# Router products among the last out-projection's, expert 0's rows in two parts, expert 1's rows among expert 0's products

## The reference

```
[u,q,k,v] = rmsnorm(x) @ w_in
x  = x + concat(pool(u), diff_attention(q,k,v)) @ w_out
h2 = rmsnorm(x)
g  = argmax(h2 @ w_group + b_group)                # 1 of 4 groups
e  = top 2 of the 4 experts of group g, by h2 @ w_erouter + b_erouter
moe = sum over the 2 chosen experts: weight * (silu(h2 @ w_gate[e]) * (h2 @ w_up[e])) @ w_down[e]
y  = rmsnorm(x + moe)
```

## Time and profile before

| what | value |
|---|---|
| three runs | 442.7, 442.85, 444.68 us; median 442.85 |
| profiled execution: span from the first to the last instruction | 441.1 us |
| median less span (what lies around the span, and scatter) | 1.75 us |
| PE busy | 416.4 us, 94% of the span |
| DVE busy | 273.4 us, 62% |
| ACT busy | 197.9 us, 45% |
| POOL busy | 124.1 us, 28% |
| mean granted TensorE clock | 0.990 of full speed |
| DMA | 91.36 MB, mean 207 GB/s; 346 to 409 GB/s in nearly all slices from 254 to 386 us |

### The profile page before, as it was taken

How to read it: one execution, slowest core, us unless ns; L and a number is a source line. 1 busy time by engine, 2 the same in 40 slices (tenths; PEclk the granted TensorE clock), 3 DMA queues, 4 the chain that set the end, 5 groups by cost and what they waited for, 6 DMA issues and landing times.

```text
span 441.1 us, 7798 instructions
## 1 busy us (share of the span) xinstructions
PE 416.4 (94%) x2932; PEld 364.6 (83%) x2933; DVE 273.4 (62%) x655; ACT 197.9 (45%) x485; POOL 124.1 (28%) x207
## 2 busy tenths in 40 slices
PE   6899999999999999999999999999999999999970
PEld 2686999997876777788886899999989999998950
DVE  2856230806769898554357898555577777659870
ACT  5476320705665756332223534444555555547340
POOL 2010000200133416242001304333344555545231
PEclk9999999999999999999999999999999999999995
DMA  8851704406000059913225699999999999984120
GB/s 269 295 179 49 227 2 128 171 1 198 2 1 3 1 212 393 369 55 145 96 97 201 192 364 392 375 409 364 348 364 346 362 346 353 366 303 151 58 78 21
DMA packets 32073, 91.36 MB, mean 207 GB/s; under 512 B 11200, under 2 KB 11712, under 8 KB 27942
## 3 DMA queue, kind: packets, MB, share of 16 engines
q1 hardware_dynamic: 20790, 71.97, 44.0%
q0 software_dynamic: 11248, 18.93, 12.1%
HBM read 86.38 MB, written 26.01 MB: 255 GB/s over the span
## 4 chain that ended last, share of the span: by engine, by line
PE 73%; DMA 11%; DVE 7%; ACT 4%; issue 3%; POOLq 0%; POOL 0%; SPq 0%; DVEq 0%; ACTq 0%
PE ps L1191 20%; PE ps L823 10%; PE ps L825 9%; PE ps L824 9%; DMA region_w<-in_w_down 5%; DMA region_x<-h_rows,lists 5%; PE ps L1208 2%; PE ps L1209 2%; PE ps L1213 2%; PE ps L1184 2%; PE ps L979 2%; PE ps L1125 2%; PE ps L944 2%; DMA region_x<-in_x_prompt 1%; PE ps L962 1%
## 5 line engine op out<-in xcount | busy, mean ns | idle before, releaser
L1191 PEld LDWEIGHTS ps<-region_p,region_a 128*128 128x128 f32 x512 | 58.2, 192 | 1.1 <-DVE region_p L2028 0.4
L1191 PE MATMUL ps<-region_p,region_a 128*128 128x128 f32 x512 | 58.6, 275 | 0.0
L825 PE MATMUL ps<-region_a_r,region_w_r 128*128 128x288 f32 x192 | 56.5, 294 | 0.0
L823 PE MATMUL ps<-region_a_r,ring_r 128*128 128x288 f32 x128 | 40.5, 317 | 0.0
L824 PE MATMUL ps<-region_a_r,ring_r 128*128 128x288 f32 x128 | 37.7, 295 | 0.0
L825 PEld LDWEIGHTS ps<-region_a_r,region_w_r 128*128 128x128 f32 x192 | 36.0, 188 | 0.0
L1578 ACT ACTIVATE region_p<-ps,gffn_sb 128x128 f32<-128x128 f32 x116 | 31.6, 384 | 8.3 <-PE ps L1184 8.3
L1599 ACT ACTIVATE region_t<-ps 128x256 f32<-128x256 f32 x16 | 6.1, 384 | 56.6 <-PE ps L1191 56.6
L1191 PEld LDWEIGHTS ps<-region_p,region_w 128*128 128x128 f32 x256 | 29.1, 192 | 1.4 <-issue 1.2
L1191 PE MATMUL ps<-region_p,region_w 128*128 128x128 f32 x256 | 29.3, 275 | 0.8 <-DMA region_w<-in_w_down 0.8
L1191 PEld LDWEIGHTS ps<-region_p,ring 128*128 128x128 f32 x256 | 29.1, 192 | 0.8 <-DVE region_p L2050 0.5
(11 more groups left out here) (358 smaller groups left out, 1022.8 us busy)
## 6 DMA issues: line engine op xcount, KB each, us to landing
region_a<-in_w_gate SPq DMA_DIRECT2D x8, 1024.0 KB, 9.6
region_a<-in_w_up SPq DMA_DIRECT2D x8, 1024.0 KB, 17.4
region_a<-in_w_down SPq DMA_DIRECT2D x8, 1024.0 KB, 18.1
region_w<-in_w_in SPq DMA_DIRECT2D x2, 2048.0 KB, 10.2
region_w<-in_w_out SPq DMA_DIRECT2D x2, 2048.0 KB, 8.0
ring<-in_w_gate SPq DMA_DIRECT2D x4, 1024.0 KB, 8.6
ring<-in_w_up SPq DMA_DIRECT2D x4, 1024.0 KB, 17.1
ring<-in_w_down SPq DMA_DIRECT2D x4, 1024.0 KB, 12.5
```

What stands on the lines that cost most here:

```text
L823: pe.matmul(out, lhs_hi, rhs_hi, start=first, stop=False)
L825: return pe.matmul(out, lhs_lo, rhs_hi, start=False, stop=last)
L1191: ins = pe.matmul(ps[:, 2 + b, (first + c) * P:(first + c + 1) * P], w[:, k, c * P:(c + 1) * P], xT[:, b, k, :], start=(k == 0), stop=(k = ...
```

## The change

- PE runs the router's products and transposes of tiles 2 and 3 earlier among the out-projection's matmuls. Six of the eight features of the last half of tile 4 go ahead of the rank matmuls of the prompt, the last two behind them. DVE and ACT evacuate to match; `residual(4, 1)` goes behind the first one-hot rows.
- Expert 0's gathered rows are plain transposes, scaled by ACT (8 chunks). The sample rows get two PSUM banks of their own (`LATE_BANK`), and DVE adds them chunk by chunk; `gate_up(0)` waits for each chunk (`first_sum`).
- The third token list and expert 1's transposes go between expert 0's groups of products; `rows_out(1)` goes ahead of the table's last steps; the first two lists go between the third and the fourth group of expert 1 (`first_lists`).
- Three `keep_running` calls go. `wd_los(0)` goes behind `lists_out(1)`; ACT's `wd_his(0)` goes behind `silu(0)`.
- Two pairs of semaphores are merged (`gains_loaded`, `ov_passed`), with the same order of work.

```diff
@@ PE, after transpose_h2(0) @@
-            for t in range(2, NT):
-                project_out(t, 0, (*heads, *pools))
-                router_logits(t - 2)
-                if t < NT - 1:
-                    project_out(t, 1, (*heads, *pools))
-                transpose_h2(t - 1)
-            project_out(NT - 1, 1, heads)
-            router_logits(NT - 2)
-            project_out(NT - 1, 1, pools)
-            pe.wait_ge(h2T_dve, PT)
-            pe.wait_ge(h2T_act, PT)
-            keep_running(2, 4)
+            project_out(2, 0, (*heads, *pools))
+            router_logits(0)
+            project_out(2, 1, (*heads, *pools))
+            transpose_h2(1)
+            project_out(3, 0, (*heads, *pools))
+            router_logits(1)
+            transpose_h2(2)
+            project_out(3, 1, heads)
+            router_logits(2)
+            project_out(3, 1, pools)
+            project_out(NT - 1, 0, heads)
+            transpose_h2(3)
+            project_out(NT - 1, 0, pools)
+            router_logits(3)
+            project_out(NT - 1, 1, (*heads, *pools[0:2]))
             pe.wait_ge(mask_ready, 1)
...
             ins.then_inc(rank_full, 1)
-            keep_running(4, 4)
-            transpose_h2(NT - 1)
-            pe.wait_ge(early_onehot, 1)
+            project_out(NT - 1, 1, pools[2:4])
+            pe.wait_ge(onehot_late, 1)
             for t in range(PT):
                 ins = pe.matmul(ps[:, 6, 0:2], onehot_all[:, 0, t, :], tokv[:, t, :], start=(t == 0), stop=(t == PT - 1))
             ins.then_inc(idx_full, 1)
+            keep_running(4, 4)
+            transpose_h2(NT - 1)
             keep_running(2, 4)
             router_logits(NT - 1)
...
             ins.then_inc(rank_full, 1)
-            keep_running(3, 4)
@@ PE, gate_up: waits by chunk, and work between the groups @@
                         for k in range(KC):
+                            if by_chunk is not None and first + c == 0:
+                                pe.wait_ge(by_chunk, k + 1)
                             ins = pe.matmul(...)
+                        for at, work in between:
+                            if at == first + c:
+                                work()
@@ PE, first_rows @@
-                for b in range(2):
-                    pe.matmul(ps[:, b, :], ones[:, :], ..., start=True, stop=False)
...
                 pe.wait_ge(xg_loaded[0], 16)
...
-                        ins = pe.matmul(..., src[:, k, :], ident[:, :], start=False, stop=(k % 4 == 3))
+                        ins = pe.transpose(..., src[:, k, :], ident[:, :])
+                pe.wait_ge(h2n_ready, NT)
+                pe.wait_ge(onehot_late, 2)
+                for k in range(KC):
+                    ins = pe.matmul(ps[:, LATE_BANK + k // 4, ...], last[:, k, :], oh_last[0:N_SAMPLE, :],
+                                    start=True, stop=True)
+                slot_tokens(0)
+                slot_tokens(1)
@@ PE, expert @@
+                if second:
+                    pe.wait_ge(xT_dve, 1)
+                if not first:
+                    pe.wait_ge(xT_act, i)
                 if first:
-                    pe.wait_ge(tab_ready, 1)
-                    for n in range(2):
-                        lists_of(n)
+                    gate_up(u, b, up_full, first_sum, ((1, lambda: slot_tokens(2)), (2, next_rows)))
+                elif second:
+                    gate_up(u, b, up_full, None, ((2, first_lists),))
+                else:
+                    gate_up(u, b, up_full)
+                if not first and (left is None or left >= 1):
+                    next_rows()
+                if second:
+                    for n in (1, 2):
                         lists_of(n)
                 if not first and (left is None or left >= EARLY):
                     lists_of(EARLY)
...
-                if first:
-                    keep_running(5, 4)
@@ ACT @@
+            (rows_out(0, k) for all 8 chunks, ahead of the Exp table)
                     ins.then_inc(xT_act, 1)
+                    if i == 0:
+                        silu(i)
+                        act.wait_ge(h2T_dve, NT)
+                        wd_his(0)
@@ DVE, routing @@
             choose(0, PT).then_inc(mask_ready, 1)
-            residual(NT - 1, 1)
             dve.wait_ge(rank_full, 1)
...
+            residual(NT - 1, 1)
             dve.wait_ge(idx_full, 1)
             dve.tensor_scalar(idx[:, EARLY:EARLY + 1], ...).then_inc(idx_ready, 1)
+            h2T_evac(NT - 1)
             h2_factor(NT - 1)
...
             expert_onehot(1)
+            for k in range(KC):
+                dve.wait_ge(first_early, k // 4 + 1)
+                dve.wait_ge(late_full, k // 4 + 1)
+                dve.scalar_tensor_tensor(xT[:, 0, k, :], late, gffn_sb[:, k:k + 1], xT[:, 0, k, :],
+                                         ALU.mult, ALU.add).then_inc(first_sum, 1)
+            to_index(0)
+            to_index(1)
...
+            dve.wait_ge(xg_transposed, 2)
+            rows_out(1).then_inc(xT_dve, 1)
             dve.wait_ge(tab_made, 1)
@@ DVE, experts @@
-            wd_los(0)
...
             for i in range(E - 1):
                 if i == 1:
                     lists_out(2)
                     lists_out(3)
-                if i == 0:
-                    dve.wait_ge(xg_transposed, 2)
-                    rows_out(1).then_inc(xT_dve, 1)
                 he_out(i)
                 if i == 0:
                     lists_out(0)
                     lists_out(1)
+                    wd_los(0)
```

More of the change, by code:

```diff
@@ L66 @@
 EARLY = 3
-TOKEN_BANK = (6, 7, 4)
+TOKEN_AT = ((6, 0), (7, 0), (6, 16))
+LATE_BANK = 3
 LISTS = 2 * RING
@@ L1165, in _ @@
             ins.then_inc(rank_full, 1)
-            keep_running(3, 4)
             def slot_tokens(i):
+                bank, col = TOKEN_AT[i]
+                pe.wait_ge(onehot_ready, i + 1)
+                pe.wait_ge(idx_ready, 1)
                 for t in range(NT):
-                    ins = pe.matmul(ps[:, TOKEN_BANK[i], 0:2], onehot_all[:, i, t, :], tokv[:, t, :], start=(t == 0), stop=(t == NT - 1))
+                    ins = pe.matmul(ps[:, bank, col:col + 2], onehot_all[:, i, t, :], tokv[:, t, :], start=(t == 0), stop=(t == NT - 1))
                 ins.then_inc(idx_full, 1)
@@ L1185, in transpose_rows, with gate_up @@
                 ins.then_inc(signal, 1)
-            def gate_up(slot, b, signal):
+            def gate_up(slot, b, signal, by_chunk=None, between=()):
                 for w, first in ((wg_sb[slot], 0), (wu_sb[slot], FC)):
@@ L1220, in first_rows @@
                 pe.wait_ge(x2_ready, 2 * NT)
-                for b in range(2):
-                    pe.matmul(ps[:, b, :], ones[:, :], tri[:, 0:1].to_broadcast([P, 512]), start=True, stop=False)
-                pe.wait_ge(oh_last_ready, 1)
-                pe.wait_ge(h2n_ready, NT)
-                for k in range(KC):
-                    pe.matmul(ps[:, k // 4, (k % 4) * P:(k % 4 + 1) * P], last[:, k, :], oh_last[0:N_SAMPLE, :],
-                              start=False, stop=False)
                 pe.wait_ge(xg_loaded[0], 16)
@@ L1531, in h2_square @@
                 for half in range(2):
-                    if t == NT - 1 and half == 1:
-                        h2T_evac(NT - 2)
+                    if t == NT - 2 and half == 1:
+                        h2T_evac(NT - 3)
                     act.wait_ge(x2_ready, 2 * t + half + 1)
@@ L1562, in _, with rows_out @@
                            scale=rs[0:N_SAMPLE, 0, PT:NT]).then_inc(h2n_ready, 1)
+            def rows_out(b, k):
+                return act.activation(xT[:, b, k, :], ps[:, k // 4, (k % 4) * P:(k % 4 + 1) * P], ACT.Copy, scale=gffn_sb[:, k:k + 1])
+            act.wait_ge(first_half, 1)
+            for k in range(4):
+                ins = rows_out(0, k)
+            ins.then_inc(first_early, 1)
+            act.wait_ge(xg_transposed, 1)
+            for k in range(4, KC):
+                ins = rows_out(0, k)
+            ins.then_inc(first_early, 1)
             act.activation(warm[:, 0:1], ones[:, 0:1], ACT.Exp)
@@ L1566, in _ @@
             act.activation(gex, gex, ACT.Exp).then_inc(gate_exp, 1)
-            act.wait_ge(first_half, 1)
-            for k in range(4):
-                ins = act.activation(xT[:, 0, k, :], ps[:, 0, k * P:(k + 1) * P], ACT.Copy, scale=gffn_sb[:, k:k + 1])
-            ins.then_inc(xT_act, 1)
             act.wait_ge(gate_in, 2)
@@ L1573, in _ @@
             act.activation(warm[:, 1:2], gmix_sb[:, 0:1], ACT.Silu)
-            def rows_out(b, k):
-                return act.activation(xT[:, b, k, :], ps[:, k // 4, (k % 4) * P:(k % 4 + 1) * P], ACT.Copy, scale=gffn_sb[:, k:k + 1])
             def wd_his(i):
@@ L2048, in _ @@
             dve.tensor_reduce(rt1[:, 3, :], diff12, X, ALU.add).then_inc(gate_in, 1)
[L2049 to L2054 removed]
+            to_index(2)
             expert_onehot(3)
```

92 lines of the change are left out of this document (45 added, 47 removed).

## The result

| | median | runs | lowest to highest |
|---|---|---|---|
| before | 443.21 us | 6 | 442.7 to 444.68 |
| after | 455.55 us | 6 | 453.57 to 456.79 |

The ratio is 1.0253, with a 95% interval of 1.0226 to 1.0279: 12.3 us slower. 449.6 was forecast, with a range of 446.0 to 453.0.

What follows compares the result with a forecast made beforehand. PE was taken as the bound, busy 94% of the span, so moving gate_up(2) moves the end; +5.4 (lists) + 2.4 (clock) - 1.0 (waits) = +6.8 us on the median 442.85 gave 449.6 us, range 446.0 to 453.0.

Steps and rivals of the forecast that it cites:

- the sum: Whole kernel: +5.4 + 2.4 - 1.0 = +6.8 us on the span of 441.1, giving 447.9 us.
- Part 4: Lists and wd_los(0): VectorE's queue delays lists_out(2), PE stands 7.0 us, gate_up(2) starts 5.4 us later.
- Part 5: Clock in PE's 7.0 us stand: falls to 1.2 GHz before down_split(0), 2.4 us lost (0 to 4.8).
- Part 2: Expert 0's rows: gathered rows first, then sample rows; gate_up(0) near 246.9 instead of 248.13, gain 1.2 us.
- The gather: Expert 0's prompt rows: starts about 239.0, takes 4.7 us, lands about 243.7; 1 us kept for the range.
- Part 3: Expert 1's transposes among expert 0's products: PE waits 0.5 us, gate_up(1) at 255.9 instead of 257.75, 1.85 us gained.
- Part 1: Router among the out-projection: mask_ready 1.0 us earlier, gather near 239.0 instead of 239.94, tile 4 0.5 to 0.6 us later.
- Part 6: Behind gate_up(2): weights come with more in hand, so 1.0 us of PE's waits is taken back (0 to 1.2).
- B: Rival: PE stands at the lists but the clock stays at 2.4 GHz, 447.2 us; chance 0.17.
- D: Rival: not slower, DVE reaches lists_out(2) before PE wants it at 264.6, 441.0 us; chance 0.13.
- C: Rival: DMA runs dry while PE stands, PE waits 3 us more for weights, 452.6 us; chance 0.10.

Runs made afterwards that it cites:

- 13 fillers: Changed kernel with 13 filler matmuls on TensorE ahead of its wait for expert 0's gathered rows: 451.37 us, ratio 1.0174.
- count_overflow alone: Changed kernel with only count_overflow moved behind the second expert's lists on VectorE: 449.19 us, ratio 1.0115.
- VectorE's order: Changed kernel with wd_los(0) ahead of lists_out(0), and wd_los(1) and count_overflow behind the later lists on VectorE: 446.77 us, ratio 1.0060.
- fillers in the long wait: Changed kernel with 30 filler matmuls on TensorE between its list products and the wait for lists_out(2): 453.09 us, ratio 1.0211.
- order and 13 fillers: Changed kernel with VectorE's order plus the 13 fillers ahead of the gathered rows: 444.43 us, ratio 1.0016.
- sample rows first: VectorE's order, with the sample rows' products and two token lists ahead of TensorE's wait for the gathered rows: 444.81 us, ratio 1.0012.
- two loads behind the gather: VectorE's order, with expert 0's w_down and expert 2's w_up loads held back until expert 0's gather has landed: 446.27 us, ratio 1.0037.
- early lists: Sample rows first, plus 4 fillers before the gather's wait and to_index(0), to_index(1), expert_onehot(2) ahead of VectorE's chunk sums: 444.00 us, ratio 1.0000.
- three fillers more: Early lists, with three more fillers behind the last rank matmuls and two fewer behind the sample rows: 442.90 us, ratio 0.9973.
- router alone: Kernel before with only the new router order up to the first gather: 444.44 us, ratio 1.0000.
- rows among (both runs): Router alone plus expert 1's transposes among expert 0's products and VectorE reordered: 444.08 us; again with three added fillers around the last tile's routing: 443.65 us.

## Why the prediction was wrong

The direction and the main mechanism were right, and the time was outside the range. The profiled execution's span is 4.1 us above the sum's 447.9: gate_up(0) starts 4.1 us too late, the stretch behind it is 0.9 longer, the next one 0.4 shorter, and 0.6 more was given back. The median lies another 1.8 us above the profiled execution. The other five executions have mean clocks of 0.960 to 0.969 and not 0.970; where they were slower is not on record.

*Part 4, right, by its own steps.* "PE stands for 7.0 us" was 6.8; lists_out(2) stands behind count_overflow; moving that one step took 3.8 us out of the wait, and moving the rest left 0.4. Read from gate_up(1), the stretch took 20.8 us where 18.8 + 2.4 was said.

*Part 5, right where it was applied.* The clock fell 5.1 us after PE's last matmul (4.8 in the earlier trace rows) and cost 2.3 us in down_split(0), said: 2.4. Fillers there gave 1.9 us of it back in the time.

*Part 2, the step that failed: "gate_up(0) then starts near 246.9 instead of 248.13, a gain of 1.2 us (0 to 2)".* It started at 250.99, 4.1 us later than that and outside its bounds. The sum took all of this work at full speed. It had the wait in hand ("they wait for the gather (243.7)") and did not ask part 5's question of it. Its own figure would not have helped: the fall 4.8 us after PE stops came from one place, behind a stretch of dense products, and the pause that it forecast here was some 2 us. The clock fell after 1.7 us in the changed kernel and, in five of the runs built on it, while PE was at work (240.3 to 244.6). The 13 fillers bring 2.5 us at gate_up(0), 3.0 at gate_up(1) and 3.5 us in the time (the ratios 1.0253 - 1.0174 = 0.0079, of 443).

*The gather, mis-sized.* "It took 4.7 us up to the load that it releases"; it took 6.7, because it now starts closer behind the 2 MB of loads. The prediction kept 1 us for this, and 1.9 was needed. It landed 1.2 us later than forecast, and the exchange of the sample rows and the gathered rows made it count: before, most of the 2 us of sample rows lay inside the flight.

*Part 3, half right.* Expert 1's transposes wait for a gather that was said to start "as before near 249.14". It started at 252.9, since to_index(0) and (1) are queued behind the chunk sums, and these behind everything that was late. In the changed kernel it still landed before PE wanted it, and PE did not wait at all where 0.5 us was forecast. The stretch took 9.9 us instead of 9.0 for the clock: 1.5 us lost in the first two groups, less the 0.5. With the 13 fillers and a full clock the late gather does show, as a wait of 0.8 us.

*Part 1, right in its direction for the prompt, and worthless.* The gather started at 238.20, 1.7 us earlier than before, where 0.9 was forecast; tile 4, said to come 0.5 to 0.6 us later, came 0.2 us earlier (its transposes start at 237.12, before at 237.36). The gain was nothing for a reason that the prediction had only in its range: the gather did not land earlier.

*Part 6.* 1.6 us were given back instead of 1.0. 1.2 of them are the two waits for DMA, of which the changed kernel has none; the other 0.4 us are not resolved. The loads of experts 3 and 4, said to start as before (253.1 and 256), went out at 257.05 and 260.85; no expert waited for them.

Of the rivals, B (the clock stays) and D (not slower) were wrong, and C (DMA runs dry) too: no expert waited for weights. With the 3.5 us of the first fall, a range up to 453 was too narrow.

## What to carry to other kernels

A step that is moved within one engine's stream moves all that stands behind it: before putting work behind a wait (here 2.4 us of it behind lists that now come later), ask which signal comes last behind it, and whom the longest small-instruction routine in that queue keeps waiting. Ask the clock's question of every place where TensorE waits, not only of the longest, and also of stretches of transposes, short products and short pauses: here the clock fell in such a stretch with PE at work. Fillers that look idle may be what holds the speed of what follows, or what brings it back; real work in the same wait did as well (444.81 against 444.43 us), and fillers behind a wait that has ended are simply in the way. A transfer that is started earlier, right behind large loads, may land no earlier: here it started 1.7 us earlier and landed 0.2 us later.

## What the runs showed of the hardware

The granted clock has two levels here, full (2.4 GHz) and half (1.2 GHz). In the profiled executions it was low between 238 and 256 as follows:

| kernel | low | TensorE just before the fall |
|---|---|---|
| changed | 243.7 to 254.0 | idle for 1.7 us |
| count_overflow alone | 244.2 to 254.4 | idle for 1.7 us |
| VectorE's order | 244.5 to 254.7 | idle for 2.9 us, then 0.1 us of transposes |
| fillers in the long wait | 240.3 to 254.0 | at work: router products and fillers |
| order and 13 fillers | 242.1 to 245.5 | at work, the same |
| sample rows first | 241.7 to 255.4 | at work, the same |
| two loads behind the gather | 240.3 to 243.7, and 250.5 to 253.9 | at work, the same; idle for 3.7 us |
| early lists | 244.6 to 248.0 | at work: the sample rows' products |
| 13 fillers alone; three fillers more | not | |
| before, router alone, rows among (both runs) | not | |

Behind dense products the clock held longer: it fell 5.1 us after the last matmul in the changed kernel (274.5), 4.1 us with the 13 fillers (270.5), 4.8 us at the end of the kernel before, and not at all in a wait of 3.0 us. In the changed kernel it stayed low for 10.2 us although TensorE was busy for the last 9 of them with transposes and small products at half speed, and for 6.8 us the second time. What decides whether it falls between 240 and 247, and for how long, no run isolates. It differed between executions: with the early lists the lowest mean clock, 0.974, went with the longest time, 447.8 us, and means of 0.987 and 0.988 with times of 442.6 to 443.0. The kernel before has such executions as well (447.87 us with a mean clock of 0.981).
